# Attention output with tokens on partitions, in a fused two-block layer kernel on one NeuronCore

## The chip, the cores and the metric

The kernel runs on one core of a Trainium2 chip. The metric is the device time of one launch in microseconds (us), median of the runs. TensorE is called PE, VectorE DVE, ScalarE ACT, GpSimd POOL and SyncE SP, as in the profile; PEld is PE's weight load. "L387" is line 387 of the kernel before.

## What is computed

A block of differential attention with a causal convolution branch and a feed-forward part, then two layers of convolution and retention. Width 1024, 512 tokens and 16 meta tokens ahead of them (528 positions), all in float32. The part that the change touches:

```python
def _diff_attention(q, k, v, lam, cid):          # 8 heads, two maps each, HEAD_DIM 64, V 128
    ...
        s = jnp.einsum('bqhmd,bkhmd->bhmqk', qb, kf)
        mask = cid[None, :] <= qc[:, None]        # chunk 0: the meta tokens; then chunks of 64
        p = jax.nn.softmax(jnp.where(mask, s, NEG_INF), axis=-1)
        a = p[:, :, 0] - lam * p[:, :, 1]
        return jnp.einsum('bhqk,bkhe->bqhe', a, vf)
...
        o = _diff_attention(q, k, v, lam, cid)
        y_att = (_rms(o, subln_w[l]) * (1.0 - lambda_init))     # rms over the 128 values of a head
        ...
        m = jax.nn.sigmoid(g_att) * y_att + jax.nn.sigmoid(g_conv) * y_conv
        h = h + m @ w_out[l]
```

## The kernel before

Each large product is made of three passes in a rounded 32-bit format: weights and activations are split into a high and a low part (`w_hi`, `w_lo`, `n_hi`, `n_lo`), and PE adds high x low, high x high and low x high. ACT rounds a 1 MB weight piece to `w_hi` (L824), DVE subtracts to get `w_lo` (L1174), and the product is at L387, over 528 positions as a piece of 256 and one of 272 columns. Activations lie with channels on partitions and positions along the free dimension.

The attention is a loop of four turns, two heads each. Ahead of the loop q and k of its heads are made; in a turn PE makes V (`v_block`, L502) with tokens on partitions, and then handles ten units: for each head one of the 16 meta positions (kind None) and four blocks of 128 queries (kinds 0 to 3), with 16, 144, 272, 400 and 528 keys. Between the steps of the units PE has 48 fill steps, each the three passes of one k-step over six matmuls (`fill`, L387), which make the gate of this turn and q and k of the next. The order on each engine is written out by hand, with semaphores.

A unit goes through these steps:

- `scores` (PE, L535, L540): both maps into the two banks of `sc`. The last block has 528 keys, 16 more than a bank holds; those 16 go to columns 256 to 271 of `tr` (L542).
- mask and maximum (DVE, L1340 to L1350), exponential with row sum (ACT, L906, L909). One or more taps of the depthwise convolution (L1258, in `conv`) fill DVE's time between.
- combination (DVE): reciprocal of both sums (L1357), second map times its reciprocal and minus lambda (L1359), first map times its reciprocal plus the second (L1362). The order of the maps is p0 - lam * p1.
- `turn` (PE, L557, L559): the combined map is transposed into `tr`, the 16 meta keys into bank 1 and the others into bank 0; ACT copies them to `atm` (16 partitions) and `at` (`copy_at`).
- `weigh` (PE, L572, L574): V as the stationary operand, the transposed map as the moving one, first a matmul over 16 meta keys and then over blocks of 128 keys. The result has V's channels on partitions and tokens along the free dimension, in bank 1 of `tr`; ACT copies it to `oT` (`copy_o`, L926).

At a turn's end the rms over a head's 128 values runs across partitions: ACT squares `oT` (L960), PE sums over partitions with twenty one-column passes for ten 128x1 matmuls (`token_sums`, L412), DVE adds epsilon (L1193), POOL raises to the power -1/2 (L329), PE spreads the factors over all partitions (`broadcast`, L422, L426), ACT copies them to `rb` (L844, L846), and DVE multiplies twice (L1379 with the norm weight, L1386 with the gate). POOL then adds the finished convolution rows to a running sum (L340), which PE sums over partitions after the last turn (L621) for the mean of the layer norm that follows; DVE divides (L1392) and PE spreads the mean (L628).

Of the kernel before, what the change touches and what calls it, by code (L numbers as in the profile page):

```python
# [24 lines left out]
P = 128  # L25
# [52 lines left out]
BC_END = ST_LAY + LAYERS * LAY_BC  # L78
# [7 lines left out]
def build(nc, io, out):  # L86
# [14 lines left out]
    with ctx:  # L101
# [24 lines left out]
        es = sb("es", [P, 2, 4])  # L126
        er = sb("er", [P, 2, 2])
# [3 lines left out]
        head_ms = sb("head_ms", [P, 8])  # L131
# [5 lines left out]
        with area:  # L137
# [19 lines left out]
            with ExitStack() as c:  # L157
# [4 lines left out]
                vm = sb("vm", [META, CW], fp32, c)  # L162
# [28 lines left out]
        at, atm = nf[:, 0, 0:NQT * P], nf[0:META, 1, 0:P]  # L191
# [13 lines left out]
        def scores_at(kb):  # L205
# [22 lines left out]
            "wo_half retm ld_decay trig cpad prep turned half_hi half_lo hsq hsum").split()}  # L228
# [76 lines left out]
        def _(pool):  # L305
# [27 lines left out]
            pool.memset(ssum[:, :], 0.0).then_inc(s["mean_all"], 1)  # L333
            with pool.Fori(0, 4) as i:
# [35 lines left out]
        def _(pe):  # L370
# [116 lines left out]
            with pe.Fori(0, 4) as i:  # L487
# [32 lines left out]
                def scores(uu):  # L520
                    hh, kind = uu // 5, KINDS[uu % 5]
                    if kind is None:
                        pe.wait_ge(s["const_done"], 4)
                    if uu == 0:
                        pe.wait_ge(evac[0], f1 + 1)
                        pe.wait_ge(evac[1], f1 + 1)
                    else:
                        pe.wait_ge(s["e_full"], unit0 + uu)
                    if kind == 3:
                        pe.wait_ge(s["at_full"], unit0 + uu - 1)  # L530
                        pe.wait_ge(s["o_full"], unit0 + uu - 1)
                    for m in range(2):
# [8 lines left out]
                        if kind == 3:  # L541
                            last = pe.matmul(tr[:, m, 2 * P:2 * P + META], qs, kT[part, hh, 512:T1],  # L542
                                             start=True, stop=True)
                    last.then_inc(s["s_full"], 1)

                def turn(uu):
# [10 lines left out]
                    last = pe.transpose(tr[0:META, 1, P:P + m], a[0:m, 0:META], ident[0:m, 0:m])  # L557
# [5 lines left out]
                def weigh(uu):  # L563
# [14 lines left out]
                pe.wait_ge(s["rb_full"], i + ST_HEADS)  # L578
# [1197 lines left out]
```

## Time and profile before

| | us |
|---|---|
| median of 3 runs | 2021.54 (2020.39 to 2023.37) |
| the profiled execution | 2022.89 |
| its span, first to last instruction | 2021.1 |
| PE busy in it | 1947.3 (96%) |
| DVE busy | 1136.4 (56%) |
| ACT busy | 651.9 (32%) |
| POOL busy | 59.3 (3%) |
| mean granted PE clock | 0.979 |

A matmul in float32 is recorded as two passes, so "x8" at L574 is four matmuls. Matmuls overlap, and their ends are modelled: the distance between two starts is the better measure of what one costs in a stream. "Granted clock" is the share of full speed (2.4 GHz) that PE got. The four turns of the attention loop begin at 152.7, 233.5, 314.0 and 394.4 us, with the first V block of each.

### The profile page before, as it was taken

What the parts mean: (1) busy time and instruction counts of PE and PEld (TensorE: products, weight loads), DVE (VectorE), ACT (ScalarE), POOL (GpSimd) and SP (SyncE); (2) the same over time, 40 slices, a digit from 0 to 9 for tenths busy, and PEclk for the clock granted to TensorE, in tenths of its full rate; (3) what the DMA queues carried; (4) which work ended last, traced back from release to release, by engine and by line L of the source; (5) the groups of instructions that cost most, each with busy time, mean ns of one, the idle gap of its engine ahead of it and who ended that gap; (6) DMA issues with size and microseconds to landing.
All of it is one profiled execution on the core that took longest, in us unless ns stands there. A gap on an engine that the chain in (4) does not pass through costs nothing.

```text
span 2021.1 us, 30306 instructions
## 1 busy us (share of the span) xinstructions
PE 1947.3 (96%) x11929; PEld 1731.2 (86%) x11929; DVE 1136.4 (56%) x1464; ACT 651.9 (32%) x1040; POOL 59.3 (3%) x67
## 2 busy tenths in 40 slices
PE   6999999999898999999989999999989999999998
PEld 6998888889898989989778888888878888888887
DVE  6777687776645544555586554445337555544522
ACT  3124343343424424424432222222323222222222
POOL 1000001101000000000010000000000000000000
PEclk7999999999998999999989999999999999999999
DMA  4221111111131332222223222332231332233231
GB/s 132 96 91 43 63 42 62 51 53 63 63 104 43 103 104 76 91 84 78 92 70 97 92 93 72 94 102 93 96 104 53 94 94 93 62 104 104 83 104 42
DMA packets 159209, 165.75 MB, mean 82 GB/s; under 512 B 2968, under 2 KB 156065, under 8 KB 159154
## 3 DMA queue, kind: packets, MB, share of 16 engines
q1 hardware_dynamic: 156648, 160.73, 25.0%
q10 hardware_dynamic: 2186, 4.20, 0.6%
q8 instruction: 38, 0.62, 0.1%
q14 instruction: 17, 0.14, 0.0%
q0 software_dynamic: 320, 0.07, 0.0%
HBM read 162.88 MB, written 2.10 MB: 82 GB/s over the span
## 4 chain that ended last, share of the span: by engine, by line
PE 60%; issue 32%; DVE 4%; ACT 2%; POOL 2%; DVEq 0%; DMA 0%; POOLq 0%; ACTq 0%
PE acc L387 50%; PE acc L693 2%; PE acc L710 2%; PE acc L502 1%; PE tr L746 1%; DVE ssum L1612 1%; POOL pw L329 1%; PE tr L422 1%; PE sc L732 1%; PE tr L574 0%; DVE w_lo L1174 0%; ACT w_hi L824 0%; PE sc L540 0%; DVE y L1258 0%; PE tr L572 0%
## 5 line engine op out<-in xcount | busy, mean ns | idle before, releaser
L1174 DVE TENSOR_TENSOR w_lo<-raw,w_hi 128x2048 fp32r<-128x2048 f32 x148 | 338.9, 2290 | 185.8 <-ACT w_hi L824 184.3
L824 ACT ACTIVATE w_hi<-raw 128x2048 fp32r<-128x2048 f32 x147 | 280.8, 1910 | 352.0 <-PE acc L387 342.1
L387 PE MATMUL acc<-n_lo,w_hi 128*128 128x256 f32 x1600 | 340.3, 294 | 11.9 <-DVE n_lo L1202 6.2
L387 PE MATMUL acc<-s_lo,w_hi 128*128 128x512 f32 x848 | 333.0, 393 | 0.0
L387 PE MATMUL acc<-s_hi,w_lo 128*128 128x512 f32 x848 | 330.3, 389 | 0.0
L387 PE MATMUL acc<-s_hi,w_hi 128*128 128x512 f32 x848 | 330.1, 389 | 0.0
L387 PE MATMUL acc<-n_hi,w_lo 128*128 128x256 f32 x1600 | 328.9, 287 | 0.0
L387 PE MATMUL acc<-n_hi,w_hi 128*128 128x256 f32 x1600 | 328.9, 287 | 0.0
L387 PEld LDWEIGHTS acc<-n_lo,w_hi 128*128 128x128 f32 x1600 | 253.8, 192 | 24.5 <-issue 19.1
L387 PEld LDWEIGHTS acc<-n_hi,w_hi 128*128 128x128 f32 x1600 | 254.8, 191 | 0.0
L387 PEld LDWEIGHTS acc<-n_hi,w_lo 128*128 128x128 f32 x1600 | 254.4, 191 | 0.0
L387 PEld LDWEIGHTS acc<-s_hi,w_lo 128*128 128x128 f32 x848 | 159.2, 188 | 33.2
L387 PEld LDWEIGHTS acc<-s_lo,w_hi 128*128 128x128 f32 x848 | 159.3, 188 | 32.2
L387 PEld LDWEIGHTS acc<-s_hi,w_hi 128*128 128x128 f32 x848 | 159.3, 188 | 32.0
L1258 DVE SCALAR_TENSOR_TENSOR y<-u,par,y (+1 forms) x240 | 168.3, 762 | 1.7 <-DVE neg_lam L1307 0.4
L1473 DVE SCALAR_TENSOR_TENSOR zy<-z,par,zy 128x528 f32<-128x528 f32 x88 | 62.6, 766 | 82.4 <-ACT zy L1034 82.4
L387 PE MATMUL acc<-m_lo,w_hi 128*128 128x512 f32 (+2 forms) x304 | 95.7, 349 | 4.4 <-DVE ob L1536 2.6
L387 PE MATMUL acc<-x_hi,w_lo 128*128 128x512 f32 x256 | 99.6, 389 | 0.0
L387 PE MATMUL acc<-x_lo,w_hi 128*128 128x512 f32 x256 | 99.6, 389 | 0.0
L387 PE MATMUL acc<-x_hi,w_hi 128*128 128x512 f32 x256 | 99.6, 389 | 0.0
L387 PE MATMUL acc<-m_hi,w_hi 128*128 128x512 f32 (+2 forms) x304 | 95.2, 347 | 0.0
L387 PE MATMUL acc<-m_hi,w_lo 128*128 128x512 f32 (+2 forms) x304 | 95.0, 347 | 0.0
(261 smaller groups left out, 2499.8 us busy)
## 6 DMA issues: line engine op xcount, KB each, us to landing
raw<-in_w_in SPq DMA_DIRECT2D x92, 1024.0 KB, 5.4
raw<-in_w_up SPq DMA_DIRECT2D x22, 1024.0 KB, 5.0
raw<-in_w_out SPq DMA_DIRECT2D x20, 1024.0 KB, 4.9
raw<-in_w_down SPq DMA_DIRECT2D x8, 1024.0 KB, 5.0
raw<-in_w_conv_out SPq DMA_DIRECT2D x4, 1024.0 KB, 5.0
decay<-in_decay ACTq DMA_DIRECT2D x8, 512.0 KB, 4.9
raw<-in_w_down SPq DMA_DIRECT2D x4, 768.0 KB, 4.3
xs<-in_x SPq DMA_DIRECT2D x4, 512.0 KB, 5.2
```

Source lines behind the costliest of these rows:

```text
L329: pool.tensor_tensor(pw[:, 0:cols], var[:, 0:cols], minus_half[:, 0:cols], ALU.pow).then_inc(s["st_pow"], 1)
L387: last = pe.matmul(acc[jj][:, bank, at_:at_ + n], w[j][:, k, jj * P:(jj + 1) * P], x[:, k0 + k, c:c + n], start=start and k == 0 and p == ...
L422: last = pe.matmul(dst[:, 0, q * P:(q + 1) * P], pw[:, n * nb + q:n * nb + q + 1].to_broadcast([P, P]), ident[:, :], start=True, stop=True)
L502: last = pe.matmul(dst, x[:, k, c:c + m], w[0][:, k, :], start=k == 0 and p == 0, stop=k == KT - 1 and p == 2)
L693: last = pe.matmul(acc[jj][:, j, :], w[j][:, k, jj * P:(jj + 1) * P], x[:, k, :], start=k == 0 and w is w_hi and x is s_hi, stop=k == KT - ...
L710: last = pe.matmul(acc[jj][:, 0, (q % 2) * CW:(q % 2 + 1) * CW], x[:, k, q * P:(q + 1) * P], w[0][:, k, :], start=k == 0 and p == 0, stop= ...
L732: last = pe.matmul(dst, rk[:, hh, kb * P:(kb + 1) * P], rq[:, hh, kb * P:SEQ], start=True, stop=True)
L746: last = pe.matmul(dst[:, q * P:(q + 1) * P], st[:, c:c + P], rv[:, kb, hh * P:(hh + 1) * P], start=kb == 0, stop=kb == q)
L824: act.activation(w_hi[j][:, :, :], raw[j][:, :, :], ACT.Copy).then_inc(hi_full[j], 1)
L1174: dve.tensor_tensor(w_lo[j][:, :, :], raw[j][:, :, :], w_hi[j][:, :, :].bitcast(fp32), ALU.subtract).then_inc(lo_full[j], 1)
L1258: dve.scalar_tensor_tensor(out=dst, in0=src, scalar=w, in1=dst, op0=ALU.mult, op1=ALU.add).then_inc(s["conv"], 1)
L1473: dve.scalar_tensor_tensor(out=zy[:, c, :], in0=z[:, c, k:k + T1], scalar=par[:, ds(tl + (C_FW + k * 44 + jj + j * FT), 1)], in1=zy[:, c, ...
```

## The change

- Weighing: the transposed map is now the stationary operand and V the moving one, so that the output has tokens on partitions and the head's 128 values along the free dimension. `atm` and `vm` have 128 partitions, of which 112 are set to zero once, so that the matmul over the meta keys spans 128 rows.
- Rms: with the values along the free dimension, ACT's square of each output piece gives the sum per token (into `ms`) as it copies it. The one-column sums, the broadcast and the copies of it are gone.
- Combination: the maps are combined as e0 - lam * (s0 / s1) * e1, with the row sums s0 and s1 and without dividing by s0; the missing factor is taken up in the rms, whose epsilon is multiplied by s0 squared. Row sums of all ten units are kept in `eu`.
- At the end of a turn DVE scales the outputs by token, PE turns them to channels on partitions (`back`: eight 128x128 and two of 16 rows) into `sc` and `tr`, and DVE multiplies them by the gate, which has taken in the norm weight beforehand. PE waits at the first scores of the next turn until that last product is done.
- The 16 keys beyond a bank are scored for the last block when the head's meta unit is scored, in free columns of `sc`, and ACT copies them to `x3` in SBUF.
- PSUM: transposed maps in bank 0 of `tr` and outputs in bank 1, except for the last block; fewer waits between the two.
- Order: after the last unit PE has ten fill steps, `back`, and three; before it had four, sums, five, broadcast, four. DVE has one tap and ten taps around its scaling, where it had two and six around the epsilon step.
- POOL sets `eu`, `ms`, `vm` and `atm` once ahead of the loop.

The core of the diff:

```diff
@@ scores (PE)
                     if uu == 0:
                         pe.wait_ge(evac[0], f1 + 1)
                         pe.wait_ge(evac[1], f1 + 1)
+                        pe.wait_ge(s["ya_full"], i * 2 + 2)
                     else:
                         pe.wait_ge(s["e_full"], unit0 + uu)
-                    if kind == 3:
-                        pe.wait_ge(s["at_full"], unit0 + uu - 1)
-                        pe.wait_ge(s["o_full"], unit0 + uu - 1)
+                    if kind is None:
+                        for m in range(2):
+                            part = slice(m * HD, (m + 1) * HD)
+                            pe.matmul(sc[:, m, CHUNK:CHUNK + META], qT[part, hh, META + 3 * P:T1],
+                                      kT[part, hh, 512:T1], start=True, stop=True)
@@ turn (PE)
-                    if uu % 5 == 3:
-                        pe.wait_ge(s["e_full"], unit0 + uu + 2)
-                    if uu > 0:
+                    if kind == 3:
                         pe.wait_ge(s["o_full"], unit0 + uu)
@@ weigh (PE)
+                    else:
+                        pe.wait_ge(s["o_full"], unit0 + uu)
-                    last = pe.matmul(tr[:, 1, 0:m], vm[:, hc], atm[:, 0:m], start=True, stop=n == 0)
+                    last = pe.matmul(tr[0:m, 1, 0:P], atm[:, 0:m], vm[:, hc], start=True, stop=n == 0)
                     for q in range(n):
-                        last = pe.matmul(tr[:, 1, 0:m], v[:, q, hc], at[:, q * P:(q + 1) * P],
+                        last = pe.matmul(tr[:, 1, 0:P], at[:, q * P:(q + 1) * P], v[:, q, hc],
                                          start=False, stop=q == n - 1)
@@ end of a turn (PE)
-                fill(4)
-                pe.wait_ge(s["head_sq"], i * 2 + 2)
-                token_sums(None, [sq[:, 0], sq[:, 1]], T1 - P)
-                fill(5)
-                broadcast(i + ST_HEADS, [tr, sc], 1)
-                fill(4)
+                fill(10)
+                back()
+                fill(3)
@@ after the last turn (PE)
-            pe.wait_ge(s["rb_full"], ST_HEADS + 4)
+            pe.wait_ge(s["ya_full"], 2 * 4 + 2)
@@ copy_o (ACT)
-                    act.activation(one(oT[:, ds(i * 2 + hh, 1), c:c + m]), tr[:, 1, 0:m],
-                                   ACT.Copy).then_inc(s["o_full"], 1)
+                    act.activation(dst, tr[0:m, 1, 0:P], ACT.Copy)
+                    act.activation(sq[0:m, 1, 0:P], tr[0:m, 1, 0:P], ACT.Square, scale=P ** -0.5,
+                                   accum_out=ms[0:m, unit_col(uu):unit_col(uu) + 1]).then_inc(s["o_full"], 1)
@@ combination (DVE)
-                    step(dve.reciprocal(er[0:m, r, :], es[0:m, r, 0:2]))
+                    step(dve.reciprocal(er[0:m, r, 1:2], eu[0:m, c, 1:2]))
                     settle()
-                    step(dve.tensor_scalar(e[0:m, r, 1, 0:end], e[0:m, r, 1, 0:end], er[0:m, r, 1:2], neg_lam[0:m, :],
+                    step(dve.tensor_scalar(er[0:m, r, 0:1], eu[0:m, c, 0:1], er[0:m, r, 1:2], neg_lam[0:m, :],
                                            ALU.mult, ALU.mult))
@@ end of a turn (DVE)
-                conv(6)
+                for hh in range(2):
+                    g_t = one(ga[:, ds(i * 2 + hh, 1), :])
+                    dve.wait_ge(evac[hh], f1 + 3)
+                    dve.tensor_scalar(g_t, g_t, 1.0, sub_w[:, :], ALU.add, ALU.mult).then_inc(s["gs"], 1)
+                conv(3)
+                dve.wait_ge(s["o_full"], unit0 + UNITS)
+                dve.tensor_tensor(head_ms[:, :], eu[:, :, 0:1].rearrange("p u o -> p (u o)"),
+                                  eu[:, :, 0:1].rearrange("p u o -> p (u o)"), ALU.mult).then_inc(s["s0sq"], 1)
+                dve.scalar_tensor_tensor(out=var[:, :], in0=head_ms[:, :], scalar=1e-6, in1=ms[:, :], op0=ALU.mult,
+                                         op1=ALU.add).then_inc(s["st_var"], 1)
                 lo(0, b1 + 2)
-                conv(2)
-                mean_square(i + ST_HEADS, 10, 1.0 / P, 1e-6)
+                conv(1)
+                dve.wait_ge(s["st_pow"], i + ST_HEADS + 1)
...
                 conv(2 * A_TAPS - taps[0])
+                dve.wait_ge(s["o_turned"], i + 1)
                 for hh in range(2):
-                    o_t = one(oT[:, ds(i * 2 + hh, 1), :])
-                    dve.scalar_tensor_tensor(out=o_t, in0=o_t, scalar=sub_w[:, :], in1=rb[:, hh, :], op0=ALU.mult,
-                                             op1=ALU.mult).then_inc(s["head_y"], 1)
+                    dve.tensor_tensor(o_t[:, 0:META], tr[:, 0, hh * META:(hh + 1) * META], g_t[:, 0:META], ALU.mult)
+                    dve.tensor_tensor(o_t[:, META:], sc[:, hh, :], g_t[:, META:], ALU.mult).then_inc(s["ya_full"], 1)
```

The order on PE around the weighing of unit 2, before; the names behind the arrow are the two operands, and `nf` holds `at` and `atm`:

```order
L387 MATMUL acc<-n_hi,w_lo 128x272
L572 MATMUL tr<-nf,vm 128x128
L574 MATMUL tr<-nf,v 128x128
L528 REGISTER_ALU
L540 MATMUL sc<-kT,qT 128x400 x2
```

and now:

```order
L407 MATMUL acc<-n_hi,w_lo 128x272
L592 MATMUL tr<-vm,nf 128x128
L594 MATMUL tr<-v,nf 128x128
L547 REGISTER_ALU
L563 MATMUL sc<-kT,qT 128x400 x2
```

The two operands have changed places, and the number of matmuls is the same. PE at the end of a turn, between fill steps, before:

```order
L422 MATMUL tr<-ident,pw 128x128 x4
L426 MATMUL tr<-ident,pw 128x16
L422 MATMUL sc<-ident,pw 128x128 x4
L426 MATMUL sc<-ident,pw 128x16
L387 MATMUL acc<-n_lo,w_hi 128x256
```

and now (`rb` and `sq` hold the outputs by token):

```order
L604 MATMUL sc<-ident,rb 128x128 x4
L605 MATMUL tr<-ident,sq 128x16
L604 MATMUL sc<-ident,rb 128x128 x4
L605 MATMUL tr<-ident,sq 128x16
L407 MATMUL acc<-n_lo,w_hi 128x256
```

The transposes of the outputs stand where the broadcast stood, and the ten one-column matmuls ahead of it have no successor. DVE at the end of a turn, from the conversion of the weights to the epsilon step, before:

```order
L1174 TENSOR_TENSOR w_lo<-raw,w_hi 128x2048
L1254 REGISTER_ALU
L1258 ISA
L1258 SCALAR_TENSOR_TENSOR y<-u,par,y 128x528
L1254 REGISTER_ALU
L1258 ISA
L1258 SCALAR_TENSOR_TENSOR y<-u,par,y 128x528
L1192 REGISTER_ALU
L1193 TENSOR_SCALAR var<-sc 128x10
```

and now, from the epsilon step (two instructions) to the scaling by token:

```order
L1407 TENSOR_TENSOR head_ms<-eu 128x10
L1409 REGISTER_ALU
L1411 SCALAR_TENSOR_TENSOR var<-head_ms,ms 128x10
L1201 REGISTER_ALU
L1202 TENSOR_TENSOR w_lo<-raw,w_hi 128x2048
L1282 REGISTER_ALU
L1286 ISA
L1286 SCALAR_TENSOR_TENSOR y<-u,par,y 128x528
L1415 REGISTER_ALU
L1416 TENSOR_TENSOR sq<-sq,pw 16x256
L1422 TENSOR_TENSOR rb<-rb,pw 128x512 x2
```

The epsilon step has moved ahead of the conversion, and one tap lies between the conversion and the scaling. Behind the last row of each piece follow six taps and the products L1379 and L1386 before, ten taps and the last products now.

## Rows read from the trace of the kernel before

**Rows 1.** The page's busy table: busy us, share of the span, instructions.

```profile
PE 1947.3 (96%) x11929; PEld 1731.2 (86%) x11929; DVE 1136.4 (56%) x1464; ACT 651.9 (32%) x1040; POOL 59.3 (3%) x67
```

**Rows 2.** Busy time by stage, the second turn: stretch, length, each engine, clock, DMA.

```profile
233.30:313.70 80.40, 76.80 (x587) 68.27 (x586) 60.27 (x108) 33.84 (x96) 5.06 (x3) 1.00 0.16 52
```

**Rows 3.** Waits of PE from 152 to 480: us in total, times, longest.

```profile
PE sc L540 <- ACT oT L926: 4.7, 8, 0.7
PE tr L557 <- ACT e L909: 4.4, 4, 1.1
```

**Rows 4.** Timeline of PE, weighing of units 1 and 9: start, busy us.

```profile
254.32 0.40 PE L387 MATMUL acc<-n_hi,w_lo 128*128 128x256 f32 x2
254.65 0.48 PE L572 MATMUL tr<-nf,vm 16*128 16x128 f32 x2
255.06 0.49 PE L574 MATMUL tr<-nf,v 128*128 128x128 f32 x2
...
297.41 1.16 PE L574 MATMUL tr<-nf,v 128*128 128x128 f32 x8
298.33 0.49 PE L387 MATMUL acc<-n_lo,w_hi 128*128 128x256 f32 x2
```

**Rows 5.** Timeline of PE, end of the second turn, with idle time and releaser.

```profile
301.34 2.29 PE L412 MATMUL sc<-ones,sq 128*128 128x1 f32 x20
303.48 0.49 PE L387 MATMUL acc<-n_lo,w_hi 128*128 128x256 f32 x2
...
308.37 1.16 PE L422 MATMUL tr<-ident,pw 128*128 128x128 f32 x8 [0.97 <-POOL pw L329]
...
310.62 0.49 PE L387 MATMUL acc<-n_lo,w_hi 128*128 128x256 f32 x2
...
314.02 0.38 PE L502 MATMUL acc<-w_hi,n_lo 128*128 128x256 f32 x1 [0.23 <-ACT kT L833]
```

**Rows 6.** Timeline of DVE, end of the second turn.

```profile
294.07 4.16 DVE L1258 SCALAR_TENSOR_TENSOR y<-u,par,y  x6
302.08 2.29 DVE L1174 TENSOR_TENSOR w_lo<-raw,w_hi 128x2048 fp32r<-128x2048 f32 x1 [3.86 <-ACT w_hi L824]
...
305.73 4.16 DVE L1258 SCALAR_TENSOR_TENSOR y<-u,par,y  x6
312.17 2.05 DVE L1379 SCALAR_TENSOR_TENSOR oT<-oT,sub_w,rb 128x528 f32 x2 [2.29 <-ACT rb L846]
```

**Rows 7.** Timeline of ACT, end of the second turn.

```profile
300.15 1.90 ACT L824 ACTIVATE w_hi<-raw 128x2048 fp32r<-128x2048 f32 x1
```

**Rows 8.** Timeline of POOL, end of the second turn.

```profile
305.89 2.42 POOL L329 TENSOR_TENSOR pw<-var,minus_half 128x10 f32<-128x10 f32 x1 [73.70 <-DVE var L1193]
...
311.65 1.33 POOL L340 TENSOR_TENSOR ssum<-ssum,y 128x528 f32<-128x528 f32 x1 [0.18 <-POOL ssum L340]
```

**Rows 9.** Groups of DVE by shape, 152 to 480: count, busy us, mean ns.

```profile
L1359 DVE TENSOR_SCALAR e<-e,er,neg_lam 128x528 f32<-128x528 f32 x8 | 4.4, 553 | 0.3
```

**Rows 10.** Timeline of ACT in the second block: squares of 128x128 with sums.

```profile
1125.31 0.28 ACT L1100 ACTIVATE sq<-tr 128x128 f32<-128x128 f32 x1 [6.91 <-PE tr L746]
...
1125.58 0.27 ACT L1100 ACTIVATE sq<-tr 128x128 f32<-128x128 f32 x1
```

**Rows 11.** Timeline of PE in the second block: eight transposes of 128x128.

```profile
1087.09 1.03 PE L753 MATMUL sc<-ident,rq 128*128 128x128 f32 x8
```

**Rows 12.** One line of DVE, a product out of PSUM: ns min, median, max.

```profile
L1669 DVE TENSOR_TENSOR cc<-acc,rb x16: 691/692/693, 1254.1 to 1880.8; 128x512 f32<-128x512 f32 x16
```

**Rows 13.** Timeline of PE after the last turn: sum for the mean, its broadcast.

```profile
474.21 1.17 PE L621 MATMUL sc<-ones,ssum 128*128 128x1 f32 x10
...
479.34 1.64 PE L628 MATMUL tr<-ident,var 128*128 128x128 f32 x10 [2.38 <-DVE var L1392]
```

**Rows 14.** Busy time by stage, two stretches of 2 us, with the granted clock.

```profile
224.00:226.00 2.00, 2.00 (x12) 2.00 (x11) 2.00 (x5) 0.00 (x0) 0.88 (x1) 0.53 0.45 127
480.00:482.00 2.00, 2.00 (x12) 2.00 (x11) 0.28 (x1) 0.67 (x2) 0.00 (x0) 0.53 0.63 206
```

More of the change, by code:

```diff
@@ L77 @@
 ST_END = ST_LAY + LAYERS * LAY_ST
-BC_END = ST_LAY + LAYERS * LAY_BC
+BC_MIX, BC_LN, BC_FFN, BC_LAY = range(4)
+BC_END = BC_LAY + LAYERS * LAY_BC
 KINDS = [None, 0, 1, 2, 3]
@@ L188, in build, with unit_col, meta_turned @@
             ob = sb("ob", [P, KT, SEQ], fp32, c)
-        at, atm = nf[:, 0, 0:NQT * P], nf[0:META, 1, 0:P]
+        at, atm = nf[:, 0, 0:NQT * P], nf[:, 1, 0:P]
+        o_rows, o_meta = rb, sq[0:META, 0]
+        def unit_col(uu):
+            hh, kind = uu // 5, KINDS[uu % 5]
+            return 8 + hh if kind is None else 4 * hh + kind
+        def meta_turned(uu):
+            return tr[0:META, 1 if KINDS[uu % 5] == 3 else 0, 3 * P:4 * P]
         acc = [ctx.enter_context(nc.psum_tensor(f"acc{j}", [P, 2, 512], fp32)) for j in range(2)]
@@ L956, in heads @@
                 copy_o(UNITS - 1)
-                act.wait_ge(s["lam_e"], 1)
-                act.wait_ge(s["o_full"], unit0 + UNITS)
-                for hh in range(2):
-                    act.activation(sq[:, hh, :], one(oT[:, ds(i * 2 + hh, 1), :]), ACT.Square).then_inc(s["head_sq"], 1)
                 hi_for(0, b1 + 2, f1 + 4)
-                rstd(i + ST_HEADS, [tr, sc], 1)
             with act.Fori(0, 3) as i:
@@ L1369, in _ @@
                         lo(1, b1 + 1)
-                conv(6)
-                lo(0, b1 + 2)
-                conv(2)
-                mean_square(i + ST_HEADS, 10, 1.0 / P, 1e-6)
+                for hh in range(2):
+                    g_t = one(ga[:, ds(i * 2 + hh, 1), :])
[3 more added lines that the diff above has]
+                dve.wait_ge(s["o_full"], unit0 + UNITS)
@@ new lines, in _ @@
+                dve.wait_ge(s["st_pow"], i + ST_HEADS + 1)
+                dve.tensor_tensor(o_meta[:, 0:2 * P].rearrange("p (h n) -> p h n", n=P),
+                                  o_meta[:, 0:2 * P].rearrange("p (h n) -> p h n", n=P),
+                                  pw[0:META, 8:10].rearrange("p (h o) -> p h o", o=1).to_broadcast([META, 2, P]),
+                                  ALU.mult).then_inc(s["o_scaled"], 1)
+                for hh in range(2):
+                    rows_h = o_rows[:, hh, 0:SEQ].rearrange("p (q n) -> p q n", n=P)
+                    dve.tensor_tensor(rows_h, rows_h,
+                                      pw[:, 4 * hh:4 * hh + 4].rearrange("p (q o) -> p q o", o=1).to_broadcast([P, NQT, P]),
+                                      ALU.mult).then_inc(s["o_scaled"], 1)
@@ L1382, in _ @@
-                for hh in range(2):
-                    o_t = one(oT[:, ds(i * 2 + hh, 1), :])
-                    dve.wait_ge(evac[hh], f1 + 3)
-                    dve.wait_ge(s["head_y"], i * 2 + hh + 1)
-                    dve.scalar_tensor_tensor(out=o_t, in0=one(ga[:, ds(i * 2 + hh, 1), :]), scalar=1.0, in1=o_t,
-                                             op0=ALU.add, op1=ALU.mult).then_inc(s["ya_full"], 1)
+                    o_t, g_t = one(oT[:, ds(i * 2 + hh, 1), :]), one(ga[:, ds(i * 2 + hh, 1), :])
```

101 lines of the change are left out of this document (61 added, 40 removed).

## The prediction

> **What bounds the kernel now.** I read the page's busy table first: TensorE (PE) is busy 96% of the span and no other engine over 56% [rows 1]. The change touches one loop, the four turns over pairs of heads, which runs from about 153 to 474 us. The table of stages gives one turn as 80.4 us, with PE busy 76.8 us and VectorE (DVE) 60.3 us [rows 2]. So a turn is PE's own stream plus the places where that stream stops. The waits of PE over the four turns name two of them: the scores of the last query block wait for ScalarE's (ACT's) copy of an earlier output, 4.7 us in 8 times, and the turning of unit 8 waits for an exponential, 4.4 us in 4 times [rows 3]. The timeline of PE at a turn's end shows the rest: twenty one-column passes for the sums of squares from 301.34 to 303.48 (2.14 us), an idle stretch until POOL's power is there at 308.37 (0.97 us in the row, 1.1 us counted from the issue of the last matmul ahead of it), then the broadcast of the 20 factors until 310.62 (2.25 us), and 0.4 us more before 314.02, because ACT first copies the broadcast and only then kT [rows 5]. None of this is product work.
>
> **The end of the turn.** Sums of squares and broadcast leave PE: 2.14 + 2.25 + 1.1 + 0.4 = 5.9 us of its stream. In their place come eight 128x128 turns and two of 16 rows. Eight turns of this kind took 0.79 us from 1087.09 to the next matmul, 1.03 us by the row's own busy time [rows 11]; the two small ones, with their changes between 16 and 128 rows (next part), I put at 0.6 us together, so 1.5 us in all, bounds 1.0 and 2.0. Net 4.4 us less per turn.
>
> **The weighing of V.** Today each unit begins with a matmul of 16 rows by the meta keys. From its start to the next matmul it takes 255.06 - 254.65 = 0.41 us, and the fill step ahead of it takes 254.65 - 254.32 = 0.33 us where such a pair of pieces otherwise takes 0.245 us (0.40 of overlapping busy time each) [rows 4]. A 128-row matmul of the same width takes (298.33 - 297.41) / 4 = 0.23 us in a chain [rows 4]. With the meta keys padded to 128 rows the first matmul should join that chain: (0.41 - 0.23) + (0.33 - 0.245) = 0.27 us for each of the eight large units, 2.2 us per turn. The two meta-only units move 128 columns now instead of 16, and give nothing. The lower bound is zero, if the 0.18 us belongs to something else than the row count; I take the 0.27 because the four-matmul chain beside it is of the same data type and width. The row shows a 16-row matmul costing more than a 128-row one. The Trainium skill has a rule for each side: TensorEngine Tiling (Array Packing), section Tiling Modes, says that changing the tiling mode drains the engine, and Performance Considerations recommends row tiling for a small contraction. By the first the saving is what the rows give; by the second padding would cost, and the sum would lose these 2.2 us per turn. The trace agrees with the first.
>
> **Waits inside the turn.** The extra 16 keys of the last block are now scored with the meta unit and kept in SBUF, so the scores of units 4 and 9 no longer wait for a copied output (4.7 / 4 = 1.2 us per turn) and the turning of unit 8 no longer waits for unit 9's exponentials (1.1 us, and about 0.25 us more at unit 3) [rows 3]. The view counts from a matmul's modelled end; between starts these three gaps are 0.1 us longer each. Two small matmuls leave and two enter. These gains are partly given back: PE arrives earlier at the same chain of DVE and ACT. Counting unit by unit from the same rows, I find about 0.6 us before the scores of unit 9 (the exponentials of unit 8), 1.0 us before the weighing of unit 8 (ACT is still in unit 9's exponentials when the turned maps are ready), and 0.5 us in small waits at units 3, 4 and 9, where the turning waits for a copy that is now followed by a square. So 2.9 gained, 2.1 returned, 0.8 net. The squares move to ACT as ten pieces: the nearest row, a square of 128x128 with its sum, goes from 1125.31 to the next in 0.27 us [rows 10], ten times 2.7 us against 1.2 + 1.6 us of squares and copies that leave; ACT is busy 34 of 80 us [rows 2] and hides it, but for those small waits.
>
> **VectorE.** Ten scalings of a whole map go (0.55 us for the largest [rows 9], 4.2 us per turn over all widths) and ten one-column operations of about 0.16 us come: 2.4 us less, which is what lets units start earlier. At the end two products of 2.0 and 1.3 us leave [rows 6] (the first at 312.17) and the gate (two, about 0.5 us each), the scaling of o by token (0.36 + 2 x 0.62) and the last products (2 x (0.15 + 0.69), by the row of a PSUM product of the same size [rows 12]) enter.
>
> **The wait that takes their place.** PE may not write the scores of the next turn until DVE has read the turned outputs out of the same bank. That is a wait of PE at the first scores of turns 2 to 4, and behind it stands all of the V projection but its first block. Both paths start at the last matmul of unit 9. DVE's: copy and square 0.8, conversion of the next weights on ACT 1.9 [rows 7], its rest on DVE 2.3, one tap 0.7, scaling 1.6, ten taps at (4.16 - 0.08) / 6 = 0.68 us [rows 6] 6.8, last products 1.7: 15.8 us. PE's: ten fill steps at 0.735, 7.4; turns back 1.5; three fill steps 2.3; first block of V 2.9: 14.1 us. PE waits 1.7 us, in three turns. POOL's power takes 2.42 us [rows 8] and ends before the conversion does, so it hides.
>
> **After the last turn.** Here DVE's ten taps after the scaling end about 2.8 us behind PE's last fill step, and POOL then adds y twice (1.33 us each with a gap [rows 8]) before PE may sum the mean. Before, PE went from its last fill step at 474.21 to the mean's broadcast at 479.34 in 5.1 us, with 2.38 us idle [rows 13]. Afterwards: 5.9 us wait, sums 1.0, two fill steps 1.6, so 8.5 us: 3.4 us more. The last turn gains 4.9 up to there, thus 1.5 net, and 0.4 us of that goes since DVE's sums then bound what PE bounded before: 1.1 us.
>
> **The clock.** In 480 to 482 us the granted clock is 0.53, between full speed (2.4 GHz) and half (1.2 GHz), behind the 2.38 us idle [rows 13, 14]; the fill pairs take 0.44 instead of 0.245 us for some 3 us, a loss of 1.3 to 1.5 us. It also falls to 0.53 at 224 to 226 [rows 14], behind the one-column sums of the first turn (and of the third); that is hidden today, since PE then only meets POOL's power without waiting, and it goes with the sums at no gain. After the 1.1 us idle in the other two turns the clock stays full. A wait of 1.7 us lies between. I charge one such fall in the three turns, 1.5 us; bounds none and three.
>
> **Sum.** Turn 1, which has no wait for a turn before it: 4.4 + 2.2 + 0.8 = 7.4 us. Turns 2 and 3: 7.4 - 1.7 = 5.7 each. Last turn with its tail 1.1. Together 19.9, less 1.5 for the clock: 18.4 us. The profiled execution took 2022.89 us (span 2021.1), 1.35 above the median of 2021.54; against it the sum gives 2004.5, against the median **2003.1 us**.
>
> **The rivals.**
> - *The padding saves nothing*: then every turn is 1.5 us longer (the 2.2, less what it had pushed into waits), 6.0 in all: 2009.1. For it: nothing but that only one kind of row is seen. 15%.
> - *Each new wait costs a clock fall*: three times 1.5 instead of once: 2006.1. For it: 1.7 is nearer to 2.38 than to 1.1. The Trainium skill, TensorE: Matmul & The Clock Gate, on oscillation, describes a loop that waits once per turn and starts cold each time. The trace shows it for one such wait. 15%.
> - *DVE's chain is longer*: a broadcast factor or the PSUM read at twice the price adds about 2 us to each of three waits and the tail: 2009. 8%.
> - *Slower*: the waits inside a turn (0.6, 1.0, 1.7 us) lie so close that PE stays at half clock for long stretches instead of 3 us. Every 10 us at half clock lose about 5 us; the gain is gone when PE spends some 40 us more at 1.2 GHz over the turns (19.9 / 0.5), and at 55 us it loses 27.5 and gives 2029.1. Against it: today's second turn has waits of 0.5 to 1.1 us, and its clock is 1.00 [rows 2]. 4%.
> - *No effect*, since waits on DVE refill what PE sheds: DVE was busy 60.3 of 80.4 us [rows 2], so it could bound a turn of 75 only if its own waits did not shrink. 4%.
>
> **How the numbers follow.** The forecast has 54%. Its range is 2000.5 to 2006. With the rivals the range that holds 8 in 10 goes from 2000.5 (no clock fall, shorter turns back) to 2010.5 (no saving by padding, and two clock falls). 0.2% is 4 us, about what a measurement of this kernel can tell from no change. Faster by more: 92%; within: 4%; slower: 4%.
>
> **What would show it.** In the profile of the changed kernel: turns of about 73, 75 and 75 us between first V blocks; no sum or broadcast passes at their ends; the first weighing matmul of a large unit 0.23 us ahead of the next; no wait of the scores of unit 4; a wait of 1 to 2 us at the first scores of turns 2 to 4, put down to DVE; some 6 us idle of PE after the fourth turn, put down to POOL. The sum is wrong if the first weighing matmul still takes 0.4 us, if the wait at the first scores is over 3 us, or if the clock is under 0.95 in the turns. Whatever lies after the mean's broadcast should keep its length.

## The result, and the profile after

The changed kernel takes 2029.5 us (median of 6 runs, 2028.0 to 2034.0) where the kernel before, run beside it, takes 2022.5 (2020.4 to 2023.4). The ratio is 1.0039, with a 95% interval of 1.0026 to 1.0052: slower by 7 us. The forecast was 2003.1 us, faster by 18. The sign is wrong, and 2029.5 lies outside the range. The profiled execution of after took 2034.0 us, the longest of the six; what it has beyond the median is found below.

The busy table of the page of after, beside [rows 1], and one turn of the loop (the second, as there) from the table of stages, beside [rows 2]:

```profile
PE 1952.3 (96%) x11809; PEld 1719.0 (85%) x11809; DVE 1137.2 (56%) x1488; ACT 653.1 (32%) x1104; POOL 60.5 (3%) x71
```

```profile
226.78:301.69 74.91, 71.67 (x559) 63.68 (x557) 60.98 (x114) 34.19 (x111) 4.84 (x3) 1.00 0.17 56
```

PE has 120 matmuls less and is busy 5 us longer. Yet the turn is 5.5 us shorter, as forecast. The waits of PE from 152 to 470 us (us in total, times, longest), beside [rows 3]:

```profile
PE sc L648 <- POOL ssum L360: 7.6, 1, 7.6
PE sc L563 <- ACT e L936: 4.1, 8, 0.8
PE tr L592 <- ACT nf L950: 3.9, 8, 0.8
PE sc L553 <- DVE oT L1432: 3.4, 3, 1.1
```

The old waits are gone, and the forecast ones stand in their place: before the scores of unit 9 and the weighing of unit 8 (0.78 and 0.80 us in the second turn), at the first scores of turns 2 to 4 (1.1 each), and after the last turn. Two small ones, 0.25 us before the scores of unit 4 and 0.19 before its weighing, make up the eight times. The prediction had written that the scores of unit 4 would not wait at all.

So the turns are not where the time went. Starts of the same work in four traces (us; e1 and e2 are the first two experiments below):

```text
start of                                      before   after   e1       e2
turn 1, first V pass                           152.7   153.1      -    152.1
turn 2, 3, 4, first V pass                     233.5   226.8      -    225.4
                                               314.0   301.7      -    300.0
                                               394.4   376.6      -    374.9
broadcast of the mean, after the loop          479.3   464.1    480.4   462.2
one-row passes of sin                          900.2   889.9    905.0   883.8
projection of the values, first               1045.3  1039.6   1051.0  1028.9
projection of the values, last                1718.1  1722.2   1733.3  1701.5
first transposes of the output                2004.4  2015.2   2026.3  1987.8
```

After leads by 15.2 us at the broadcast of the mean, by 10.3 at 900, and is 10.8 behind at the end. All of the lead of 15.2 us was lost in code that the change does not touch. The timeline of PE shows how, in one of these stages. Before, then after (start, busy us):

```profile
1299.63 0.39 PE L387 MATMUL acc<-s_hi,w_hi 128*128 128x512 f32 x1
1299.85 0.39 PE L387 MATMUL acc<-s_hi,w_lo 128*128 128x512 f32 x1
1300.08 0.39 PE L387 MATMUL acc<-s_lo,w_hi 128*128 128x512 f32 x1
```

```profile
1299.54 0.40 PE L407 MATMUL acc<-s_hi,w_hi 128*128 128x512 f32 x1
1299.77 0.40 PE L407 MATMUL acc<-s_hi,w_lo 128*128 128x512 f32 x1
1300.01 0.40 PE L407 MATMUL acc<-s_lo,w_hi 128*128 128x512 f32 x1
```

Over some 80 such starts from 1300 us on, the mean distance is 0.2267 us before and 0.2323 after, 2.5% more. The table of stages says the same for 100 us in which PE never waits and the granted clock is 1.00, 443 passes before and 432 after:

```profile
1300.00:1400.00 100.00, 100.00 (x443) 82.81 (x442) 47.58 (x51) 26.23 (x24) 0.00 (x0) 1.00 0.30 94
```

```profile
1300.00:1400.00 100.00, 100.00 (x432) 81.08 (x431) 45.96 (x50) 25.13 (x23) 0.00 (x0) 1.00 0.31 94
```

These matmuls, their operands and their order are the same in both kernels. What differs is where the tensors lie. The change adds `eu`, `ms` and `x3` and lengthens `head_ms`, all allocated ahead of the large activation tensors; with rounding these move up by 384 bytes per partition (`n_hi` and `s_hi` from 100992 to 101376). The weight tiles `w_hi` and `w_lo` lie ahead of them and stay (`w_hi` at 32896).

### The profile page after: what moved, and what is told of

It is laid out like the page before. It is cut to its first block, busy times and chain, and to the rows that moved or that the text cites. A ratio compares the mean times of both kernels' runs of the same rounds, so it can differ in the third digit from the quotient of the medians.

```text
span 2032.0 us, 30143 instructions
## 1 busy us (share of the span) xinstructions
PE 1952.3 (96%) x11809; PEld 1719.0 (85%) x11809; DVE 1137.2 (56%) x1488; ACT 653.1 (32%) x1104; POOL 60.5 (3%) x71
## 4 chain that ended last, share of the span: by engine, by line
PE 63%; issue 26%; DVE 6%; ACT 3%; POOL 1%; DVEq 0%; DMA 0%; POOLq 0%; ACTq 0%
PE acc L407 51%; PE acc L522 2%; PE acc L720 2%; PE acc L737 2%; PE tr L773 1%; ACT e L936 1%; DVE y L1286 1%; DVE ssum L1657 1%; PE sc L563 1%; DVE w_lo L1202 1%; PE tr L594 1%; PE sc L759 1%; ACT w_hi L851 1%; PE tr L442 0%; POOL pw L343 0%
## 5 line engine op out<-in xcount | busy, mean ns | idle before, releaser
L407 PE MATMUL acc<-s_lo,w_hi 128*128 128x512 f32 x848 | 337.4, 398 | 0.0
L407 PE MATMUL acc<-s_hi,w_lo 128*128 128x512 f32 x848 | 334.5, 394 | 0.0
L407 PE MATMUL acc<-s_hi,w_hi 128*128 128x512 f32 x848 | 334.5, 394 | 0.0
```

The source lines that it names most:

```text
L407: last = pe.matmul(acc[jj][:, bank, at_:at_ + n], w[j][:, k, jj * P:(jj + 1) * P], x[:, k0 + k, c:c + n], start=start and k == 0 and p == ...
```

## The experiments

### Are the addresses the cause?

**e1**: the kernel before, only its tensors moved.

```diff
         es = sb("es", [P, 2, 4])
+        gap = sb("gap", [P, 96])
         er = sb("er", [P, 2, 2])
```

> The kernel before with one unused tile of 384 bytes per partition put where the change puts its new small tiles, so that every large tensor from n_hi on lies 384 bytes higher, at the addresses of the kernel after (n_hi at 101376 in place of 100992). No instruction changes. Theory A (the 128x512 matmuls of the unchanged stages went from 0.227 to 0.232 us apart because the tensors moved): their distance is again 0.232 us at 1300 us and the time is about 2022 + 25 = 2047 us, since the loop gains nothing here. Theory B (the distance comes from how the earlier end of the loop lines the stages up with the transfers and with the other engines) and theory C (from where the instructions of the changed program lie): 0.227 us and 2022 us, no change. Between 2030 and 2040 both have a part.

**e2**: the kernel after, its small tiles behind `e`, where nothing else lies; `head_gap` keeps the hole.

```diff
-        eu = sb("eu", [P, UNITS, 4])
-        ms = sb("ms", [P, UNITS])
-        x3 = sb("x3", [P, 2, META])
...
-        head_ms = sb("head_ms", [P, UNITS])
+        head_gap = sb("head_gap", [P, 8])
...
                 e = sb("e", [P, 2, 2, T1], fp32, c)
+                eu = sb("eu", [P, UNITS, 4], fp32, c)
+                ms = sb("ms", [P, UNITS], fp32, c)
+                x3 = sb("x3", [P, 2, META], fp32, c)
+                head_ms = sb("head_ms", [P, UNITS], fp32, c)
```

> The kernel after with its new small tiles (eu, ms, x3, head_ms) put behind e, in bytes that no other tensor uses, so that every large tensor has the address it had before. No instruction changes against the kernel after but the addresses. Theory A: the 512-column matmuls are 0.227 us apart again and the time is that of the sum of the prediction, 2003 to 2007 us. Theories B and C: 0.232 us and 2029.5 us, as the kernel after.

Measured: e1 2044.9 us (2044.5 to 2045.2), ratio to before 1.0111 (1.0094 to 1.0128), 22.6 us slower by an unused tile. e2 2005.3 us (2004.4 to 2006.6), ratio 0.9914 (0.9898 to 0.9931). The same 100 us, of e1 and then of e2:

```profile
1300.00:1400.00 100.00, 100.00 (x432) 81.08 (x431) 47.58 (x50) 25.11 (x23) 0.00 (x0) 1.00 0.31 94
```

```profile
1300.00:1400.00 100.00, 100.00 (x443) 82.81 (x442) 46.80 (x50) 24.96 (x22) 0.00 (x0) 1.00 0.33 104
```

Both go with theory A and against B and C. The loss is 22.6 us with the loop of before and 2029.5 - 2005.3 = 24.2 with that of after. In e2 the lead is 17.1 us at the broadcast of the mean and 16.6 at the output: with the addresses held, what lies after the loop keeps its length.

### Which addresses?

**e3, e5, e8, e11, e12, e16, e17, e18** are e2 with one unused tile of 128, 256, 64, 32, 192, 224, 96 and 160 bytes ahead of `n_hi`. **e6** has 128 bytes there and 128 ahead of `w_hi`, **e7** only those ahead of `w_hi` (which move the activations too). The diff is that of e6; the width of `area_gap` is the number of bytes by four.

```diff
+        w_gap = sb("w_gap", [P, 32])
         w_hi = [sb(f"w_hi{j}", [P, KT, CW], f32r) for j in range(2)]
...
+        area_gap = sb("area_gap", [P, 32])
         area = ExitStack()
```

> The kernel of e2 with 128 unused bytes ahead of n_hi: the large tensors lie 128 bytes above their addresses of before instead of 0 (e2) or 384 (after). If theory A holds, this tells what about the address counts: if only the 1024-byte boundary that the shift by 384 reaches is bad (101376 is a multiple of 1024), it stays at e2's time, 2003 to 2007 us; if any odd multiple of 128 is as bad as 384, it is at 2029. By B and C it is at 2029.5.

> The kernel of e2 with 256 unused bytes ahead of n_hi. The large tensors then lie 256 bytes above their addresses of before (n_hi at 101248, an odd multiple of 128, as 100992 was; after 384 or 128 bytes it is an even one). Theory A1 (what counts is whether the moving operand of the matmul starts on a multiple of 256 bytes): 0.227 us between the 512-column matmuls and 2003 to 2007 us. Theory A2 (any move away from the old distance to the weights, w_hi at 32896, is bad): 0.232 us and 2028 us.

> The kernel of e2 with 128 unused bytes ahead of w_hi and 128 more ahead of n_hi: the weights' split tiles now start on multiples of 256 bytes (33024), while n_hi and what lies behind it are at odd multiples of 128 (101248), as in e5. If the moving operand alone counts (A1), the matmuls with stationary weights stay at 0.227 us, and those of the retention values' projection, whose moving operand is the weights, go from 288 to some 295 ns: within 3 us of e2. If what counts is that both operands have the same remainder by 256 (A3), 0.232 us and 2026 to 2030 us. If the stationary operand prefers a multiple of 256 (the projection's rows in e1 went from 288 to 283 ns as its stationary slices moved there), below e2, down to 1995 us.

> The kernel of e2 with 128 unused bytes ahead of w_hi and none ahead of n_hi: weights at 33024 and n_hi at 101120, both multiples of 256. A1 (the moving operand must not start on a multiple of 256): 0.232 us and 2028 us. A3 (both operands need the same remainder): 0.227 us and 2003 to 2007 us.

> The kernel of e2 with 64 unused bytes ahead of n_hi (101056, remainder 192 by 256, 64 by 128). If only the two remainders 0 and 128 differ in kind, this tells which side 192 is on: 2003 to 2007 us if only a start on a multiple of 256 is slow, 2028 us or more if anything but the old remainder is slow; in between if the loss is in proportion to the distance.

> The kernel of e2 with 32 unused bytes ahead of n_hi: a difference of 32 between the operands' remainders by 256. The times at 0, 64 and 128 were 2005.3, 2010.1 and 2027.9 us. A loss in steps of 64 bytes: 2005 us; a loss that grows with the distance: 2006 to 2008 us; a start off a multiple of 64 bytes bad in itself: 2030 us or more.

> The kernel of e2 with 192 unused bytes ahead of n_hi: 192 above, or 64 below the weights' remainder by 256. If the loss is symmetric, 2010 us as with 64 above; if it grows through the whole circle, over 2030 us.

> The kernel of e2 with 224 unused bytes ahead of n_hi, 32 below the weights' remainder by 256. If what counts is a difference that is a multiple of 64 against one that is an odd multiple of 32: 2023 us as with 32. If a larger address by a little is bad and a smaller one good: 2005 us. 192 below 256 (e12: 2025 us) says neither.

> The kernel of e2 with 96 unused bytes ahead of n_hi. Odd multiples of 32 so far cost the 512-column passes 6 ns (32: 0.233, 224: 0.233): 0.233 us and 2020 to 2032 us. If only distances near 0 on the upper side are good (0 and 64), 0.230 us and some 2012 us.

> The kernel of e2 with 160 unused bytes ahead of n_hi: 0.233 us between the 512-column passes and 2020 to 2032 us by both readings. A value at 0.227 would mean that there is no order in it.

Measured. The difference is that of the start addresses of activations and weights, by 256. "512" is the mean distance of passes with 512 moving columns from 1300 us on, "pair" that of two passes with 256 and 272 columns on `n_hi` and `n_lo` over some 70 starts from 115 to 133 us, one longer step of 0.35 us in each included; without it every value is some 1.5 ns lower:

```text
difference   run          time us    512, ns   pair, ns
0            e2, e5, e7   2004.8 to 2005.8   227   246
32           e11          2022.8             233   242
64           e8           2010.1             229   245
96           e17          2034.9             233   248
128          e3, e6       2027.9, 2029.7     232   248
160          e18          2027.9             234   242
192          e12          2025.3             233   242
224          e16          2031.9             233   248
```

e3, e5, e6 and e7 are four corners: activations moved by 128 alone, by 256 alone, weights by 128 and activations by 256, both by 128. The two with equal remainders are good and the two with unequal ones bad. So neither operand's own address counts (A1 falls), nor the absolute distance (A2 falls), but the difference of the two by 256 (A3). e6 and e7 also differ in nothing that lies ahead of `n_hi`, so the own addresses of the raw weights, `h` and the small tiles are out as a cause. What lies between the weights and `n_hi` moved together with the weights in both, so its distance to the activations was not held apart; these passes don't read it. I know of no order in the other six differences. The expectations for 32 and 192 missed, and for 96 the distance of 0.233 us came as expected, but the time of 2034.9 lies above the 2020 to 2032 that were given; 224 and 160 came at the 0.233 and 0.234 us of one of their readings, 224 with 2031.9 us where that reading had 2023. The single runs of e12 spread from 2016.8 to 2026.3, wider than any other.

The groups by shape show that the preference belongs to the form of the pass. The projection of the values has activations as the stationary and weights as the moving operand. Before and then e1 (count, busy us, mean ns):

```profile
L710 PE MATMUL acc<-w_hi,s_hi 128*128 128x256 f32 x256 | 73.8, 288 | 0.0
...
L387 PE MATMUL acc<-s_hi,w_hi 128*128 128x512 f32 x848 | 330.1, 389 | 0.0
```

```profile
L711 PE MATMUL acc<-w_hi,s_hi 128*128 128x256 f32 x256 | 72.0, 281 | 0.0
...
L388 PE MATMUL acc<-s_hi,w_hi 128*128 128x512 f32 x848 | 334.5, 394 | 0.0
```

Its rows are shorter by 7 ns with the tensors moved, while those of the 512-column passes are longer by 5. A row's own time is not its price, so I take the distance between starts: over 758 steps of this projection it went from 123.6 to 119.4 ns, 3.2 us in all. The common step is 0.120 us in both kernels, but before has 31 steps of some 0.2 us and e1 has 2. At a difference of 64 (e8) the common step is 0.114 us. The Trainium skill, SBUF — State Buffer, section Who interferes with whom, gives PE two independent read ports, for the moving operand and for the weight load, and says that it never waits on anyone. By that a shift should cost nothing; these runs measured 22 to 24 us. Whether the weight load and the moving stream meet somewhere in the memory was only guessed: the profile has no row for it.

### The terms of the sum

**e4** is e2 with the meta keys' product from 16 rows again in the eight large units; the two small units keep 128.

```diff
-                    last = pe.matmul(tr[0:m, 1, 0:P], atm[:, 0:m], vm[:, hc], start=True, stop=n == 0)
+                    rows = P if kind is None else META
+                    last = pe.matmul(tr[0:m, 1, 0:P], atm[0:rows, 0:m], vm[0:rows, hc], start=True, stop=n == 0)
```

> The kernel of e2 with the weighing of the meta values from 16 rows of both operands again for the eight units that also have values of 128 rows (the two meta units keep 128). My sum counts 0.27 us for each of these eight passes: 2.2 us in a turn, 8.6 us in all, so e2's time + 6 to 9 us; the row of the fill pair that follows or precedes goes from 0.22 to 0.35 us again. The rival that padding saves nothing: e2's time within 1 us.

Measured: 2012.1 us (2010.1 to 2013.2), 6.8 more than e2 and within the 6 to 9 expected. Its turns are 74.6, 76.0 and 76.1 us against 73.3, 74.6 and 74.9, so 1.3 more each. The waits say where the rest of 2.2 went, e2 first and then e4:

```profile
PE sc L564 <- ACT e L937: 4.3, 8, 0.8
```

```profile
PE sc L564 <- ACT e L938: 0.8, 4, 0.2
```

PE waits 3.5 / 4 = 0.9 us less per turn for the exponentials when its own passes are slower, and 1.3 + 0.9 = 2.2.

### Can the tail be had back?

**e9, e10, e15**: e2 with 12, 13 and 11 of the 31 taps ahead of the loop in place of 10 (`G_TAPS = 12`, 13, 11).

> The kernel of e2 with 12 in place of 10 of a tile's 31 convolution taps done before the attention loop: four taps of some 0.7 us leave each turn of the loop, all four from the row of ten ahead of the head's last multiplication, and go ahead of it. In e2's trace the PE waits for that multiplication 3.8 us in three turns and 7.6 us for the column sums after the last turn, both behind these ten taps. If VectorE's taps are what these waits come from (as my account of the tail says), the three waits go and the last one shrinks by 2.7 us: 6 us less than e2, 1999 us, less up to 2 us if VectorE then is late ahead of the loop (16 taps more, 11 us, against 24.8 us that it waits there). Rival: the last wait is GpSimd's two additions (4.4 us) at a fixed place and the early waits return elsewhere: e2's time within 1 us.

> As e9 with 13 taps ahead of the loop: two more of each turn's last four. If the taps are the bound of the tail, 1 to 2 us below e9; if VectorE ahead of the loop has become late, above it.

> The kernel of e2 with 11 taps ahead of the loop. With 12 (e9), the waits at the turns' starts (3.8 us) went and the one after the last turn shrank by 4.6, but three waits of 5.4 us for VectorE came ahead of the loop. Two taps (1.5 us) fit in the 2.1 us that VectorE waits in each of those stages in e2, four do not: so the early waits should stay under 1 us and the time go 3 to 5 us below e2, 2000 to 2002 us. Rival, that what is gained at the loop is lost again whatever the number: 2005 us.

Measured: e9 2005.7 us (2003.9 to 2006.1), e10 2007.8 (2006.7 to 2011.4), e15 2001.9 (2001.2 to 2002.7). The waits of PE from 60 to 500 us in e9 show why 12 bring nothing:

```profile
PE acc L408 <- DVE u L1323: 5.4, 3, 1.9
...
PE sc L649 <- POOL ssum L361: 3.0, 1, 3.0
```

The wait after the last turn fell from 7.6 to 3.0 and those at the turns' starts are gone (3.8 in e2), but 5.4 us (0.4 in e2) came ahead of the loop, where VectorE is now late. The expectation had put this at up to 2, so the time it gave, 1999 us, was missed. With 13 the early waits are 9.5 us and the last one still 1.8, which is slower than e9, as the second reading of e10 had it. With 11 the three early waits together are 1.4 us, where under 1 was expected, and the gain of 3.4 us stays.

**e13, e14**: `n_hi` and `n_lo` alone moved by 32 bytes, all behind them by 256; e14 has 11 taps as well.

```diff
+            sb("n_gap", [P, 8], fp32, area)
             n_hi = sb("n_hi", [P, KT, ROW], f32r, area)
             n_lo = sb("n_lo", [P, KT, ROW], f32r, area)
+            sb("m_gap", [P, 56], fp32, area)
```

> The kernel of e2 with n_hi and n_lo alone moved by 32 bytes (101024) and all that lies behind them by 256; s_hi, s_lo, x_hi and x_lo stay where they were. With every tensor moved by 32 (e11), the pairs of a 272- and a 256-column matmul on n came every 0.242 us instead of 0.246 while the 512-column ones went from 0.227 to 0.233. If each form of pass goes by the addresses of its own two operands: pairs at 0.242, 512-column ones at 0.227, and about 2400 pairs times 4 ns = 10 us less than e2, less what those stages wait on others: 1996 to 2000 us. If the tensors lose together, 2010 to 2023 us.

> e13 with 11 taps ahead of the loop in place of 10. If both gains stand and add up: e13 less 2 to 5 us.

Measured: e13 2001.8 us (1999.6 to 2003.9), 3.5 less than e2 and not 5 to 9. Both distances came out as expected (pairs 242 ns, 512-column passes 227), so each form of pass does go by its own operands. What was missed is V, whose stationary operand is `n_hi`: its 480 passes came every 0.117 us instead of 0.114 where nothing interrupts them, 1.4 us back. The pairs' gain also doesn't show in the turns: the first and third take 73.4 and 74.7 us against 73.3 and 74.9 in e2, so what PE saves there returns as waits or in V. The second takes 76.4 against 74.6, because in the profiled execution (2003.9 us, the longest of the four) the granted clock was 0.50 from 229.1 to 232.5 us, behind a wait of 1.35 us at the first scores. How the rest of the gap to 10 divides is not settled. e14: 1997.1 us (1994.4 to 1999.3), ratio to before 0.9876 (0.9859 to 0.9892), 4.7 below e13. It beats both kernels.

## Why the prediction was wrong, and where it was right

**The step that failed** is the last sentence of "What would show it": that whatever lies after the mean's broadcast should keep its length. Nothing in the sum had a term for it, and no rival asked what the change does to code that it leaves alone. The passes with 512 columns went from 0.2267 to 0.2323 us. There are 3 x (848 + 256) + 144 = 3456 of them in the second block: 19.4 us. The projection of the values gave 2.8 us back (123.6 to 120.0 ns in after). In after the stretch from 900 us to the output grew by 21.1 us, in e1 by 17.1. The 4 us between the two lie ahead of the projection, and most of them are a fall of the clock that this one execution of after has and those of before and e1 have not. The table of stages, before and then after:

```profile
900.00:910.00 10.00, 9.85 (x74) 9.09 (x75) 8.31 (x16) 0.86 (x1) 0.00 (x0) 1.00 0.01 2
```

```profile
890.60:897.40 6.80, 6.80 (x30) 6.13 (x29) 5.68 (x11) 0.03 (x1) 0.00 (x0) 0.50 0.01 2
```

6.8 us at half speed lose 3.4, and the execution was 4.4 us above after's median: this part is not the addresses. 19.4 - 2.8 + 3.4 = 20.0 of 21.1 us, and 19.4 - 3.2 = 16.2 of 17.1 in e1; 1 us stays open in each. Another 5 us had gone between the broadcast and 900 us (3.7 in e1, 0.7 in e2).

**The sum itself**, read in after:

- Turns: forecast 7.4, 5.7, 5.7 us gained; measured 80.8 - 73.7 = 7.1, 5.6 and 5.5. In e2, with the addresses of before, 7.5, 5.9 and 5.5.
- End of the turn, turns back for 1.5 us. PE's timeline, beside [rows 5]:

```profile
297.94 0.60 PE L604 MATMUL sc<-ident,rb 128*128 128x128 f32 x4
298.47 0.23 PE L605 MATMUL tr<-ident,sq 16*128 16x16 f32 x1
298.63 0.66 PE L604 MATMUL sc<-ident,rb 128*128 128x128 f32 x4
299.21 0.23 PE L605 MATMUL tr<-ident,sq 16*128 16x16 f32 x1
```

From 297.94 to the next fill pair at 299.37 is 1.43 us, and that pair takes 0.35 instead of 0.245: 1.5 us.

- Padding. The weighing of unit 1 and what stands around it, beside [rows 4]:

```profile
249.08 0.41 PE L407 MATMUL acc<-n_hi,w_lo 128*128 128x256 f32 x2
249.32 0.38 PE L592 MATMUL tr<-vm,nf 128*128 128x128 f32 x2
249.54 0.39 PE L594 MATMUL tr<-v,nf 128*128 128x128 f32 x2
249.86 0.94 PE L563 MATMUL sc<-kT,qT 64*128 64x400 f32 x4
```

The fill pair takes 0.24 us instead of 0.33 and the meta keys' matmuls 0.22 instead of 0.41: 0.28 for this unit, forecast 0.27. The matmul over its other keys also shortens, from 0.42 (255.06 to 255.48 before) to 0.32, which the forecast had not counted. And the eight units are not alike: by the distances in e4 and e2, four gain 0.32 to 0.40 us and four 0.19 to 0.20, where the fill pair gains nothing. That eight times the price of unit 1 came near the 2.26 us of the eight together is luck. e4 shows 2.2 us per turn on PE and 1.3 net. The rival "padding saves nothing" put the net at 1.5 and is out.

- Waits returned inside the turn: forecast 2.1 us, measured (4.1 + 3.9) / 4 = 2.0.
- First scores of turns 2 to 4: forecast 1.7 us, measured 1.1 (1.1 to 1.4 in the experiments with ten taps), behind DVE's ten taps (297.53 in DVE's timeline, beside [rows 6]):

```profile
297.53 6.86 DVE L1286 SCALAR_TENSOR_TENSOR y<-u,par,y  x10
304.33 0.15 DVE L1431 TENSOR_TENSOR oT<-tr,ga 128x16 f32 x1
304.41 0.67 DVE L1432 TENSOR_TENSOR oT<-sc,ga 128x512 f32 x1
```

- The clock: I charged 1.5 us for one fall in the turns. There was none; the granted clock is 1.00 in every stretch of 2 us around the three waits of 1.1. The rival of a fall at each wait is out, too: fourteen kernels here have three such waits each, and 2 of the 42, in e13 and e18, were followed by a fall, of 3.4 us at half speed.
- The tail was sized worst: 1.1 us gained was forecast, 2.6 lost was measured (87.5 us from the fourth turn's start to the broadcast, 85.0 before). PE's timeline, beside [rows 13]:

```profile
451.25 0.41 PE L407 MATMUL acc<-n_hi,w_lo 128*128 128x256 f32 x2
459.22 2.27 PE L648 MATMUL sc<-ones,ssum 128*128 128x1 f32 x10 [7.56 <-POOL ssum L360]
461.35 0.79 PE L407 MATMUL acc<-n_lo,w_hi 128*128 128x256 f32 x2
...
464.13 2.15 PE L655 MATMUL tr<-ident,var 128*128 128x128 f32 x10
```

The wait is 7.6 us where I had 5.9, the sums take 2.1 where I had 1.0, and the two fill steps 2.8 where I had 1.6: 4.0 us over. The last two terms are the clock (half speed, 0.50 in the table of stages):

```profile
452.00:454.00 2.00, 0.00 (x0) 0.00 (x0) 2.00 (x4) 2.00 (x2) 0.00 (x0) 0.93 0.00 0
454.00:456.00 2.00, 0.00 (x0) 0.00 (x0) 2.00 (x6) 0.17 (x1) 1.35 (x2) 0.50 0.00 0
...
464.00:466.00 2.00, 2.00 (x12) 2.00 (x11) 0.00 (x0) 0.00 (x0) 0.00 (x0) 0.50 0.00 0
```

I had priced the short waits with a fall and left the long one without. The first term is POOL's second addition, which I took at 1.33 us [rows 8]. In the timelines of POOL and DVE:

```profile
454.47 1.30 POOL L360 TENSOR_TENSOR ssum<-ssum,y 128x528 f32<-128x528 f32 x1 [10.94 <-DVE y L1286]
455.95 3.12 POOL L360 TENSOR_TENSOR ssum<-ssum,y 128x528 f32<-128x528 f32 x1 [0.18 <-POOL ssum L360]
```

```profile
455.50 2.42 DVE L1202 TENSOR_TENSOR w_lo<-raw,w_hi 128x2048 fp32r<-128x2048 f32 x1
```

It lies beside a long subtraction of DVE's, which ends at 457.92, and takes 3.12 us; after the other turns, beside taps, it took 1.57. The Trainium skill, SBUF — State Buffer, section Who interferes with whom, says that a VectorE instruction with two inputs in SBUF contends with a GpSimd one that reads it, over a pair of ports that is locked for one of them. The trace is near that: from 455.95 to the end of the subtraction are 1.97 us, together with the 1.30 us of the first addition an estimate of 3.3. The taps have two inputs in SBUF as well, but last 0.69 us and not 2.42. Moving the subtraction was not tried.

Together after leads by 15.2 us at the broadcast where the sum had 18.4, and e2 by 17.0 at the end: 2005.3 us. With the addresses held, the forecast would have been 2 us off. A part of that is luck: the tail was off by 3.7 us, and the 1.5 us charged for a clock fall in the turns, which did not come, made up for some of it.

## What to carry to other kernels

When a change adds even a few bytes of on-chip memory, write down the addresses of the large operands before and after, and give the case that they move a term and a rival of its own; put new small tiles behind the large ones. A stage that the change doesn't touch is compared by the distance between its matmuls' starts, since a busy share of 100% hides 2.5%; a matmul's own time in the trace is no measure of it, as the 7 ns of the projection show. Look for a clock fall that only one of two executions has before their difference is put down to the change. Price a clock fall at the long wait first, and when work is moved ahead of a loop, count the slack of the engine that receives it, per stage.

## What the runs showed of the hardware that I had not expected

- In these runs the distance between matmuls in 32-bit format goes with the difference of the start addresses of moving and stationary operand by 256 bytes: 0.227 us at 0, 0.229 at 64, 0.232 to 0.234 at the six others for 512 moving columns, 443 against 432 passes in 100 us. Pairs of 256 and 272 columns are fastest at 32, 160 and 192 (242 ns against 245 to 248), while the projection of the values is slowest at 0 (124 ns in the mean against 118 to 121 elsewhere). The whole kernel moves between 2004.8 and 2034.9 us by it.
- A matmul with 16 contraction rows inside a stream of 128-row ones costs the stream 0.19 to 0.40 us more than one padded to 128 rows (0.28 in the mean of eight places): 0.09 to 0.20 on itself, some 0.1 on the 128-row matmul behind it in seven of the eight, and in four of the eight 0.09 on the pair ahead.
- Waits of 1.1 to 1.4 us in a busy stream left the granted clock at 1.00 in 40 of 42 cases, and in two (1.35 and 1.38 us) 3.4 us at 0.50 followed. The wait after the last turn was 7.6, 6.4, 6.3, 3.0 and 1.8 us in after, e14, e15, e9 and e10; the clock was at 0.50 for 13.7, 10.2, 6.8, 6.8 and 3.4 us during and behind it, in after from 453.7 to 467.4.
- A POOL addition of 128x528 took 3.12 us beside a DVE subtraction of 2.42 us, 1.57 beside convolution taps of 0.69 us and 1.30 beside products that read PSUM; subtraction and taps both have two inputs in SBUF.
